# Start of a transformer-like backbone: modulation in eight chunks of 256 columns, four input and thirteen modulation buffers, bias table added by VectorE

## What is computed

```python
sh1, sc1, gt1, sh2, sc2, gt2 = adaln(c, w_mod, b_mod)          # silu(c) @ w_mod + b_mod, six slices of 2048
csh1, csc1, ...              = adaln(c_ctx, w_mod, b_mod)
hx = rms_norm(x, g_mix) * (1 + sc1) + sh1
hc = rms_norm(ctx, g_mix) * (1 + csc1) + csh1
x_pool, x_u, x_v, x_lru, x_lg, x_q, x_k, x_val = split(hx @ w_in)   # and the same for hc
... attention: s_loc = q.k * scale + bias(rpb), masked columns -1e30; s_ctx = q.k_ctx * scale
... four mixers, gates, output projection, SwiGLU feed-forward, rms_norm
```

## Time and profile before

| | us |
|---|---|
| median of 3 runs | 1672.09 (1671.12 to 1672.24) |
| profiled execution | 1670.43 |
| its span in the trace | 1668.8 |
| PE busy | 1622.0 |
| DVE busy | 1089.8 |
| ACT busy | 727.9 |
| POOL busy | 158.5 |

### The profile page before, as it was taken

How to read it: one execution, slowest core, us unless ns; L and a number is a source line. 1 busy time by engine, 2 the same in 40 slices (tenths; PEclk the granted TensorE clock), 3 DMA queues, 4 the chain that set the end, 5 groups by cost and what they waited for, 6 DMA issues and landing times.

```text
span 1668.8 us, 22482 instructions
## 1 busy us (share of the span) xinstructions
PE 1622.0 (97%) x7707; PEld 1319.9 (79%) x7707; DVE 1089.8 (65%) x1222; ACT 727.9 (44%) x796; POOL 158.5 (10%) x294
## 2 busy tenths in 40 slices
PE   4899999999999999999999999999999999999998
PEld 2467888987778888888878788888888888888876
DVE  2424335777788888778977667767765556456477
ACT  4324234547744444434445644443444444434434
POOL 1002001000012212123110001101100000000000
PEclk9899999999999999999999999999999999999999
DMA  9997447554469979899676568778776666666654
GB/s 357 384 368 220 130 131 229 173 178 144 154 225 330 328 262 326 291 316 344 245 252 215 151 215 266 256 234 282 238 268 192 189 190 189 189 196 189 179 164 139
DMA packets 183862, 389.09 MB, mean 233 GB/s; under 512 B 14368, under 2 KB 14608, under 8 KB 182912
## 3 DMA queue, kind: packets, MB, share of 16 engines
q1 hardware_dynamic: 160784, 312.63, 57.9%
q0 software_dynamic: 23024, 75.74, 13.2%
HBM read 385.30 MB, written 3.01 MB: 233 GB/s over the span
## 4 chain that ended last, share of the span: by engine, by line
PE 89%; DVE 5%; DMA 3%; ACT 2%; issue 1%; SPq 0%; DVEq 0%; ACTq 0%
PE ps L1347 24%; PE ps L1349 24%; PE ps L1348 24%; PE ps L1319 4%; PE ps L1321 4%; PE ps L1320 4%; PE ps L1400 2%; PE ps L1315 2%; DVE LO L767 1%; DMA MR<-in_w_mod 1%; DMA RAW<-in_w_in 1%; ACT HI L436 1%; DMA BR<-in_w_mod 0%; PE ps L1523 0%; PE ps L1509 0%
## 5 line engine op out<-in xcount | busy, mean ns | idle before, releaser
L767 DVE TENSOR_TENSOR LO<-RAW,HI 128x1024 fp32r<-128x1024 f32 x504 | 614.7, 1223 | 432.2 <-ACT HI L436 430.7
L436 ACT ACTIVATE HI<-RAW 128x1024 fp32r<-128x1024 f32 x504 | 533.0, 1060 | 789.1 <-PE ps L1349 672.5
L1347 PE MATMUL ps<-HI,H 128*128 128x512 f32 x1872 | 734.8, 393 | 6.7 <-DVE LO L767 3.7
L1349 PE MATMUL ps<-HI,H 128*128 128x512 f32 x1872 | 729.6, 390 | 0.0
L1348 PE MATMUL ps<-LO,H 128*128 128x512 f32 x1872 | 729.3, 390 | 0.0
L1347 PEld LDWEIGHTS ps<-HI,H 128*128 128x128 f32 x1872 | 351.9, 188 | 83.7 <-issue 7.4
L1349 PEld LDWEIGHTS ps<-HI,H 128*128 128x128 f32 x1872 | 351.9, 188 | 73.7
L1348 PEld LDWEIGHTS ps<-LO,H 128*128 128x128 f32 x1872 | 351.9, 188 | 73.1 <-issue 1.2
L400 POOL DMA_DIRECT2D BR<-in_w_mod x224 | 120.4, 538 | 773.1 <-DVE BR L864 315.2
L864 DVE SCALAR_TENSOR_TENSOR BR<-BR,SCF 128x512 f32<-128x512 f32 (+1 forms) x210 | 156.7, 746 | 8.4 <-DMA BR<-in_w_mod 7.1
L1319 PE MATMUL ps<-H,HI 128*128 128x256 f32 (+1 forms) x384 | 126.4, 329 | 0.0
(11 more groups left out here) (252 smaller groups left out, 792.4 us busy)
## 6 DMA issues: line engine op xcount, KB each, us to landing
RAW<-in_w_gate SPq DMA_DIRECT2D x128, 512.0 KB, 4.8
BR<-in_w_mod POOLq DMA_DIRECT2D x224, 256.0 KB, 4.5
RAW<-in_w_ffn_gate SPq DMA_DIRECT2D x88, 512.0 KB, 3.8
RAW<-in_w_ffn_up SPq DMA_DIRECT2D x88, 512.0 KB, 3.8
RAW<-in_w_ffn_down SPq DMA_DIRECT2D x88, 512.0 KB, 3.7
RAW<-in_w_in SPq DMA_DIRECT2D x64, 512.0 KB, 4.6
RAW<-in_w_branch SPq DMA_DIRECT2D x32, 512.0 KB, 5.0
RAW<-in_w_out SPq DMA_DIRECT2D x32, 512.0 KB, 4.5
```

What stands on the lines that cost most here:

```text
L436: act.activation(HI[:, j % RING, :], RAW[:, j % RING, :], ACT.Copy).then_inc(hi_done, 1)
L767: tt(LO[:, j % RING, :], RAW[:, j % RING, :], HI[:, j % RING, :], ALU.subtract).then_inc(lo_done, 1)
L1347: mm(o, xh, wh, start=first and t == 0, stop=False, skip_group_check=True)
L1349: i = mm(o, xl, wh, start=False, stop=last and t == 1, skip_group_check=True)
```

## The change

**Chunks.** Scale and shift are computed together, in eight chunks of 256 columns. A modulation piece is now 512 rows by 256 columns (still 512 KB); scale and shift pieces alternate. `mod_unit` multiplies one of each: eight matmuls of 256 columns. A second stationary table `SHP` holds silu(c) two columns further on, so that the shift's sums fall on other rows of the same bank. One copy (256 columns), one turn (two matmuls of 4 columns with the wider `PICK`) and one set of columns (two bias adds, one combination) serve a chunk, and after each chunk one group of 256 channels of `H` is made.

**Buffers.** Modulation pieces have thirteen buffers: `RAWX`, `MR`, `ACCM`, and eight in the space of `XTOK`, which SP may fill once PE has turned the token tile that lay there (`x_turned`). All four buffers of `RAW` belong to the input pieces, and the values' pieces follow on in the same ring.

**Tokens.** Root, reciprocal and scaling go tile by tile; PE turns tile 0 ahead of the first modulation unit and one tile after each of the next three. The table for the square root is loaded once ahead.

**Order of products.** Keys and queries pieces alternate (`input_units`); 16 groups of three matmuls are dealt per chunk.

**Elsewhere.** The bias table is added by DVE in the bank, ahead of the row maximum, and line 1510's matmul goes. `LRU_AT` moves one piece ahead, the last gate of the first block too; the copy of the queries goes from `w` = 19 to 18. At the end, `gate2_rows` goes to 11 and 13 and `final_add` to 14, 16, 18 and 22.

```diff
-START = []
...
-MOD_RING = 7
-ROWS_TURNED = (0, 0, 4, 10, 16)
+CHUNKS, CW = 8, 2 * P
+CHUNK_INPUTS = [(2 * c - 1, 2 * c) if c else (0,) for c in range(CHUNKS)]
+INPUT_AT = [{2: 2 * c - 1, 6: 2 * c} if c else {6: 0} for c in range(CHUNKS)]
+INPUTS = [("queries" if p % 2 else "keys", p // 2) for p in range(2 * CHUNKS)]
+DEAL = [(5, 3, 5, 3) if c > 1 else (0, 3, 5, 3) for c in range(CHUNKS)]
+MOD_RING = 13
...
-LRU_AT = (67, 74, 81, 88)
+LRU_AT = (66, 73, 80, 87)
...
+            slots = [RAWX[:, j, :] for j in range(3)] + [MR.rearrange("p s e -> p (s e)"), ACCM.rearrange("p s e -> p (s e)")]
+            slots += [BR[:, j * PC:(j + 1) * PC] for j in range(8)]
+            return slots[p % MOD_RING]
...
+        v_mod = w_mod[0].rearrange("(q t p) n -> p q t n", t=4, p=P)
...
+            def mod_piece(ch, j):
+
+                p, col = 8 * ch + j, (1 - j % 2) * D + ch * CW
                 if p >= MOD_RING:
                     sp.wait_ge(s("mod1_used"), p - MOD_RING + 1)
+                elif p >= 5:
+                    sp.wait_ge(s("x_turned"), 4 * ((p - 5) // 2 + 1))
+                sp.dma_start(mod_raw(p).rearrange("p (t n) -> p t n", n=CW), v_mod[:, j // 2, :, col:col + CW])\
+                    .then_inc(mod1_landed[p % MOD_RING], 16)
...
+            for ch in range(CHUNKS):
+                for j in range(8):
+                    if j in INPUT_AT[ch]:
+                        input_piece(INPUT_AT[ch][j])
+                    mod_piece(ch, j)
+            input_piece(15)
...
+            for ch in range(CHUNKS):
+                for p in CHUNK_INPUTS[ch]:
+                    high(0, p)
+                act.wait_ge(s("mod1_used"), 8 * ch + 8)
+                if ch:
+                    act.wait_ge(s("mod1_turned"), ch)
+                act.activation(MROW, ps[:, 6, 0:CW], ACT.Copy).then_inc(s("mrow"), 1)
+                act.wait_ge(s("mod1_read"), ch + 1)
+                input_context(ch)
+                input_high(ch)
...
-                if w == 17:
-                    evac_win(0)
-                if w % 8 == 3 and w < 68 and w != 35:
+                if w in (17, 18):
+                    evac_win(w - 17)
+                if w % 8 == 3 and 19 < w < 68 and w != 35:
...
+            for ch in range(CHUNKS):
+                for p in CHUNK_INPUTS[ch]:
+                    low(p, p % RING)
+                mod1_columns(ch)
+                input_float(ch)
+                input_low(ch)
+            low(15, 15 % RING)
...
                             dve.wait_ge(s("scores"), 4 * half + u + 1)
+                            own.did(tt(masked, masked, TB[:, h, 2 - 2 * t:6 - 2 * t, :], ALU.add)); own.wait()
                             dve.reduce_max(ST[:, 8 + u:9 + u], ps[:, 4 + u, :], AX_X, negate=True).then_inc(s("row_max"), 1)
...
-                if w in (7, 8):
-                    gate2_rows(w - 7)
-                if w == 9:
+                if w in (11, 13):
+                    gate2_rows((w - 11) // 2)
+                if w == 14:
                     dve.wait_ge(s("down_read"), 4 * (FC - 1))
-                if w in (9, 10, 13, 15):
-                    final_add((9, 10, 13, 15).index(w))
+                if w in (14, 16, 18, 22):
+                    final_add((14, 16, 18, 22).index(w))
...
+            def mod_unit(ch, i):
+
+                p = 8 * ch + 2 * i
+                if i == 0 and ch:
+                    pe.wait_ge(s("mrow"), ch)
+                for part in range(2):
+                    pe.wait_ge(mod1_landed[(p + part) % MOD_RING], 16 * ((p + part) // MOD_RING + 1))
+                for part, silu in enumerate((SCP, SHP)):
+                    for g in range(4):
+                        m = mm(ps[32 * g:32 * g + 32, 6, 0:CW], silu[:, 4 * i + g, :], mod_raw(p + part)[:, g * CW:(g + 1) * CW],
+                               start=i + part == 0, stop=i == 3 and part == 1, skip_group_check=True, tile_position=(0, 32 * g))
                 m.then_inc(s("mod1_used"), 2)
...
+            for ch in range(1, CHUNKS):
+                for i in range(4):
+                    mod_unit(ch, i)
+                    deal(DEAL[ch][i])
+                mod1_turn(ch)
...
-                            mm(o, QT[:, h, t * P:t * P + P], KTT[:, h, :], start=True, stop=False, skip_group_check=True)
-                            mm(o[:, T:2 * T], IDENT, TB[:, h, 2 - 2 * t:6 - 2 * t, :], start=False, stop=True,
-                               skip_group_check=True).then_inc(s("scores"), 1)
+                            mm(o, QT[:, h, t * P:t * P + P], KTT[:, h, :], start=True, stop=True, skip_group_check=True)\
+                                .then_inc(s("scores"), 1)
```

More of the change, by code:

```diff
@@ L1379, in params_turn @@
                 turn(ps[:, 5, 0:PB_N], PBROW).then_inc(s("params_turned"), 1)
-            def rows_turn(b):
-                pe.wait_ge(s("rows_scaled"), b // 4 + 1)
-                if b >= 4:
-                    pe.wait_ge(s("xt_dve" if b % 2 else "xt_act"), b // 2 - 1)
-                for k in range(4):
-                    kk = b % 4 * 4 + k
-                    m = turn(ps[:, b % 4, k * P:k * P + P], XTOK[:, b // 4, kk * P:kk * P + P], start=k == 0)
-                m.then_inc(s("x_turned"), 1)
@@ L1404, in mod1_turn, with rows_turn @@
-            def mod1_turn(q, part):
-                pe.wait_ge(s("mrow"), 2 * q + part + 1)
-                pe.wait_ge(s("params"), 1)
-                if q + part:
-                    pe.wait_ge(s("mod1_read"), 2 * q + part)
-                for k in range(4):
-                    c = 64 + 16 * q + 8 * part + 2 * k
-                    m = mm(ps[:, 7, c:c + 2], MROW[:, part * BW + k * P:part * BW + (k + 1) * P], PICK,
-                           start=True, stop=True, skip_group_check=True)
+            def rows_turn(tile):
+                pe.wait_ge(s("rows_scaled"), tile + 1)
+                for b in range(4):
+                    if tile:
+                        pe.wait_ge(s("xt_dve" if b % 2 else "xt_act"), 2 * tile - 1 + b // 2)
+                    for k in range(4):
+                        kk = 4 * b + k
+                        m = turn(ps[:, b, k * P:k * P + P], XTOK[:, tile, kk * P:kk * P + P], start=k == 0)
+                    m.then_inc(s("x_turned"), 1)
@@ L1414, in mod1_turn, with input_units @@
+            def mod1_turn(ch):
+                pe.wait_ge(s("mrow"), ch + 1)
+                if ch == 0:
+                    pe.wait_ge(s("params"), 1)
+                else:
+                    pe.wait_ge(s("mod1_read"), ch)
+                for k in range(2):
+                    a = 64 + 4 * (2 * ch + k)
+                    m = mm(ps[:, 7, a:a + 4], MROW[:, k * P:(k + 1) * P], PICK, start=True, stop=True, skip_group_check=True)
                 m.then_inc(s("mod1_turned"), 1)
-            def keys(q):
-                for j in range(2):
-                    p = 4 * q + j
-                    pe.wait_ge(s("h_lo"), 2 * q + j + 1)
+            def input_units():
+                for p, (kind, q) in enumerate(INPUTS):
+                    pe.wait_ge(s("h_lo"), q + 1)
@@ L1428, in keys @@
                             yield
-            def queries(q):
-                for j in range(2):
-                    p = 4 * q + 2 + j
-                    if q + j == 0:
-                        pe.wait_ge(s("params"), 1)
-                    ready(p)
-                    for t in range(2):
-                        k = 4 * q + 2 * j + t
-                        for f in range(4):
-                            o, opens = halves(4)(f)
-                            i = rows3(o, *weights(p, t, f), *only_x(k), k == 0 and opens, k == KT - 1)
-                            if t == 1 and f == 3:
-                                i.then_inc(used, 1)
-                            yield
-            def keys_and_queries():
-                for q in range(4):
-                    yield from keys(q)
-                    yield from queries(q)
-            work = keys_and_queries()
+            work = input_units()
             def deal(n):
```

209 lines of the change are left out of this document (74 added, 135 removed).

## The result

The changed kernel takes **1661.47 us** (median, 1659.89 to 1662.88) where the kernel before took 1672.16 beside it: ratio 0.994, 95% interval 0.9927 to 0.9953. The forecast was 1661.0. The profiled execution took 1659.89 us with a span of 1658.2, where before it was 1670.43 and 1668.8.

A forecast was written before the change was run, and what follows sets the result against it. PE bound the kernel: a late start beside full transfers, then nonstop work. Start -4.7, values -1.7, bias table -3.0 and end -1.5 made -10.9 from 1672.09, so 1661.2, stated as 1661.0; range 1655 to 1667.

The forecast's parts named there:

- What bounds: Whole kernel: PE's work behind the start; in the start, PE starting late ended last, beside transfers done at about 125 us.
- Part 1: Head start: keys begin behind 12 modulation pieces, not 22, at about 39.5 us, 15 us earlier, though transfers then bound.
- Part 2: Price of transfers in the start: 1 KB rows at 359 GB/s, 1.46 us a piece, last modulation piece landing at 133.0.
- the other end, 294 GB/s: Low bound for the 1 KB rows' rate, from a stretch of mostly 512-byte rows on q0: 1.78 us a piece.
- Part 3: Work behind the last modulation piece and PE's pace: start ends at 148.0, not 153.35, -5.4 us, -4.7 with lag.
- The lag: PE in the start: waits and slow clock leave it behind the transfers, 0.7 us of that remaining at the end.
- Part 4: At the values: PE's wait for the queries' copy goes, through earlier values' pieces and copy: -1.7 us, at worst 0.
- Part 5: Scores: eight bias-table matmuls leave PE, 3.4 us, less 0.4 us of wait behind DVE's additions: -3.0 us.
- The 0.4 us set off for the piece behind the second scores: Behind the second scores: DVE's additions eat 1.9 us of 1.5 us cover, so PE waits 0.4 us.
- Part 6: Kernel's end: spreading gate rows and residual adds gives -1.5 us, bounds -1.9 and +1; LRU branch earlier gives nothing.
- PE can't follow: Rival on the start: units cost 1.2 us, slow clock's 4 us never won back; 1663.7 to 1666, chance 0.20.

The follow-up runs named there:

- rows_512: Changed kernel with each modulation piece read as 8 x 128 columns (rows of 512 bytes), sums from wrongly placed weights: 1684.12 us, ratio 1.0076.
- rows_2k: Changed kernel with each modulation piece read as 2 x 512 columns (rows of 2 KB), sums from wrongly placed weights: 1653.9 us, ratio 0.9896.
- deal_last: Changed kernel dealing 5, 3, 4, 2 product groups in the last chunk in place of 5, 3, 5, 3: 1659.4 us, ratio 0.9931.
- copy_19: Changed kernel with the queries' copy back at position 19 instead of 18: 1664.7 us, ratio 0.9965.
- table_by_pe: Changed kernel with the bias table added by PE's matmul again instead of by DVE: 1663.94 us, ratio 0.9958.
- end_close: Changed kernel with the second gate's rows and the residual adds back at positions 7 to 15: 1663.83 us, ratio 0.996.
- start_only: Kernel before with only the changed start and the queries' copy one position earlier: 1667.59 us, ratio 0.9981.
- ring_7: Changed kernel with 7 modulation buffers in place of 13: 1661.11 us, ratio 0.9941.
- lru_late: Changed kernel with the LRU branch and the first block's last gate copy one position later again: 1660.29 us, ratio 0.9941.
- after_again: The changed kernel run once more, unaltered, as the measure for two runs beside it: 1660.72 us.
- both: Changed kernel with the last chunk dealing 5, 3, 4, 2 groups and the LRU branch one position later again: 1661.15 us, ratio 0.9936.
- late_14: Changed kernel reading input piece 14 behind the last modulation piece, last chunk dealing 5, 3, 3, 2 groups: 1659.36 us, ratio 0.9931.

## Why the prediction was right, point by point

**What bounds.** Right: PE's late start was the bound before, transfers and the fixed work behind the last piece are now.

**Part 1.** First keys at 41.27, forecast 39.5 and at most 41. The second chunk's unit waited for its piece until 39.40 and then took 1.94 us, most of it at half clock (the granted clock is 0.78 from 30 to 40 us and 0.87 from 40 to 50). It cost nothing as far as the traces show: from 60 us on PE waits for transfers.

**Part 2, the mis-sized term.** The rate of rows of 1 KB: 349 GB/s in place of 359, 1.50 us a piece in place of 1.46. The straight line through rows of 8 and 2 KB left a fixed 6.6 ns for each row of a DMA engine; a row of 1 KB took 16 x 1024 / 349 = 46.9 ns where the line gives 45.7. Sixty-four pieces make 2.6 us of it: 133.0 + 2.6 = 135.6, where the piece landed. That the other end, 294 GB/s, was of 512-byte rows is not to be seen in the earlier trace rows, where a packet of q0 is 3.6 KB on average; rows_512 measured that size itself. The estimate from the Trainium skill, "DMA: Bandwidth & Descriptors", section "Why small descriptors are slow (HBM only)", was 368 GB/s, further off in the same direction. The same page of the Trainium skill, "Specifications", gives 512 B as the least size for line rate; the traces contradict it on this queue, with 387, 349 and 289 GB/s for rows of 2 KB, 1 KB and 512 B (the last two worked out from mixes of 356 and 304).

**Part 3.** The fixed work is right: 15.12 us from the last unit's start to the values, forecast 15.0. So is PE's pace: 13.60 us a chunk in rows_2k, forecast 13.8 (the sum named a dropped turn of 0.93 us, which it didn't subtract and which isn't dropped: a half round has one turn before and now). The lag is 0.6, forecast 0.7, but that is chance. The forecast had PE still behind from the slow clock of the 30s and 40s; in fact it had caught up and stood for pieces, and came late to the last one because five groups of keys were dealt ahead of it (deal_last). The small gaps forecast for PE between 50 and 130 us are there, 5.9 us in 70 from 60 on, at a clock of 1.00.

**Part 4.** Right, 1.7 us, but for another reason than I gave first: the copy's place on ScalarE did it alone (copy_19).

**Part 5.** 3.0 was taken; table_by_pe says 2.8 in the trace and 2.5 to 3.0 in the medians. The 0.4 us set off for the piece behind the second scores was paid: the lead over table_by_pe falls by that much at 296.61, though the list of waits doesn't show it. Another 0.4 us at 318.93 was not foreseen.

**Part 6.** The end gave its whole 1.9 us of waits where 1.5 was taken, and 2.5 by end_close; by the starts of the matmuls it is even 2.9, beyond the bound of 1.9 (below). The LRU branch was put at nothing: 1.5 us less of waits in the traces, at most that in the runs.

What the parts behind the values gave can be read at one matmul that all kernels share, and at PE's last matmul. The two in the kernel before, then in after:

```profile
915.37 2.05 PE L1713 MATMUL ps<-ATT,BR 128*128 128x128 f32 x16 [0.59 <-DVE ATT L1147]
1660.37 0.39 PE L1321 MATMUL ps<-HI,H 128*128 128x512 f32 x1
```
```profile
907.66 2.05 PE L1685 MATMUL ps<-ATT,BR 128*128 128x128 f32 x16 [0.59 <-DVE ATT L1141]
1649.81 0.39 PE L1315 MATMUL ps<-HI,H 128*128 128x512 f32 x1
```

| | from the values to that matmul | from there to PE's last matmul |
|---|---|---|
| before | 762.0 | 745.0 |
| start_only | 760.8 | 745.0 |
| table_by_pe | 759.0 | 742.2 |
| after | 756.3 | 742.2 |
| end_close | 755.9 | 745.0 |

The end is thus worth 2.9 us, and the 5.7 in front of it are the table's 2.7, the copy's 1.2 to 1.7 and, as what is left, 1.3 to 1.8 for the LRU branch. All five lost 1.7 us of clock in the LRU stage, so that falls out.

So the sum: start 2.0, and behind it 5.7 + 2.9 = 8.6 us. The start was taken 2.7 us too large and the rest 2.4 too small, and it is luck that the two errors cancel to 0.5 us. Three of the signs set down beforehand missed narrowly, all in the start: first keys at 41.27 (38 to 41), the last piece at 135.6 (131 to 135), the values at 151.36 (147 to 150). And the 2.0 us rest on one trace of the kernel before: with the lost clock put back, the eight executions of the changed start lie 1.1 to 2.4 us ahead of it. Of the rivals "PE can't follow" lands nearest in time (1663.7) but not in cause: PE kept its pace and waited for pieces.

## What to carry to other kernels

When a change starts a stage earlier, look for the next bound and price it in the size of its own rows: here 13 us of earlier keys were worth 8.2 us with rows of 2 KB, where PE's own pace bounds, and 2.0 with rows of 1 KB, because each modulation piece became 11% dearer. Behind the last piece count the fixed chain, and send for nothing ahead of that piece that can't be used before its chain is done. A part's price when it is undone isn't its gain when it is made: a returned wait can cost clock that the old one did not. And the list of waits understates a loss: line up the starts of the matmuls of two runs.

## What the runs showed of the hardware

Waits of about 2 us in the middle of dense work sometimes cost 1.7 us of clock and sometimes nothing. Of ten profiled executions with 2.1 us of idle time ahead of H's last rows, six lost it (ring_7, rows_512, table_by_pe, lru_late, copy_19, start_only) and four did not (after, after_again, end_close, rows_2k); none of the three did in which that gap was 1.0 to 1.4 us (deal_last, both, late_14). In the LRU stage a wait of 1.9 to 2.0 us cost it in eight profiled executions and not in after_again and rows_2k; of four with 2.6 us, before and start_only lost it, lru_late and both did not. Where the clock fell, it did so between 0.1 us ahead of PE's return and 1.2 us behind it, and each time it cost 1.7 us. What decides it stays open, and with it a part of the spread of 3 to 4 us between runs of one kernel.

The rates of one queue by row size, all with the engines full: 8 KB 405 to 417 from 5 to 10 us, 2 KB 386 to 387, 1 KB with a fifth of 2 KB rows 355 to 356 (349 alone, worked out), 512 B with a fifth of 2 KB rows 289 to 309 GB/s.
